# Turning the head-norm output in two halves, and projecting it by halves of its features

## The chip, the core and the metric

The kernel runs on one core of a Trainium2 chip: one TensorE (PE in the profile), one VectorE (DVE), one ScalarE (ACT), one GpSimd (POOL), and one queue (SP) that issues all weight transfers. Time is measured on the device in microseconds (us), from start to end of the program. All arithmetic is in 32-bit floats.

## What is computed

The model is a stack of two blocks on 256 tokens of width 1024. The change touches the mixers of the first block, which run twice (once for each of its two layers). A mixer has two branches, retention and a gated delta rule ("gdn"). In the delta rule a unit lower-triangular system is solved per head. Cut to what matters here:

```python
def mixer_block(h, ...):
    u = rmsnorm(h, g_norm)
    proj = u @ w_in                      # all projections, and two gates mg_ret, mg_gdn
    ...
    y_ret = (o.reshape(B, T, RET_V) * silu(rg)) @ w_br_ret
    ...
    beta = sigmoid(gb)
    g = -exp(a_log) * softplus(ga + dt_bias)
    o = gated_delta_rule(q, k, v, g, beta)                        # 8 heads of 128 features
    o = o * rsqrt(mean(o * o, axis=-1) + EPS) * gdn_gn            # norm of each head
    y_gdn = (o.reshape(B, T, GDN_V) * silu(gz)) @ w_br_gdn        # 1024 x 1024
    merged = sigmoid(mg_ret) * y_ret + sigmoid(mg_gdn) * y_gdn
    return h + merged @ w_out                                     # 1024 x 1024
```

`w_br_gdn` contracts over 1024 features, 128 for each head: features 0 to 511 come from heads 0 to 3, and 512 to 1023 from heads 4 to 7.

## The kernel before

Activations are held transposed, as 8 tiles of 128 features x 256 tokens. Weights stream from memory in slabs of 512 rows x 512 columns (1 MB) through a ring of six (`ring`). PE waits for a slab in `take_slab`; the SP queue issues the transfer of slab n once slab n-6 has been used, in the order of one list (`slab_list`). A projection with transposed output (`linear_t`, matmuls at L413) makes 512 output columns from two slabs: first with features 0 to 511 of the input, then with 512 to 1023. That is 16 matmuls for each slab. Each 32-bit matmul leaves two records in the trace; a transpose leaves one. PSUM is used as four buffers (`ps0` to `ps3`), taken in turn by `take_unit`.

There is no planner: each engine's program is written out by hand, and semaphores tie the engines together. The end of a mixer runs like this:

- `solve_pe`, `solve_dve` and the loops of `mixer_act` and `mixer_pool` handle the heads in two halves of four. For every head n, GpSimd first makes a spread operand (`spread`, L1210: a copy of decay sums and beta over 128 columns into one of two buffers `bc`), PE multiplies it (`spread` at L777 to L780), DVE turns that into a decay mask and the scaled keys (`decay`, L1121 to L1123), and PE makes the Gram matrices (`gram`, L787 to L790). Beside this, PE works through pieces of independent projections (`beside_pe`, L413).
- After the levels of the solve come four short products, u1, r, u2 and o (L833 to L854); each waits for another engine. The last makes the output `o` of four heads in PSUM.
- The head norm follows: ACT squares (L933), DVE sums (L1177) and scales (L1178), GpSimd takes the power -1/2 (L1190), DVE multiplies by it (L1181) and by the gate (L1186) into `o_gdn`. After the second half only, an empty DVE instruction raises `nat_ready`.
- In the second half of the solve GpSimd's first two spread operands stand behind its L1190 of the first half.
- `turn_pe` (L513) then transposes `o_gdn`, 8 transposes for features 0 to 511 and 8 for the rest, into two PSUM buffers. DVE (`turn_dve`, L523) and ACT (`turn_act`, L536) copy one each to `oT`, with the gain. PE waits for both copies.
- PE projects by `w_br_gdn` in two column groups of two slabs each, which DVE gates and adds (`merge_dve`, L1085 and L1087; one `merged_out` for each group). PE waits for both of them, and projects by `w_out`.

`bc` copies wait for `kb_out`, so that a buffer is not overwritten while it is read. The lines named here are the profile's.

Of the kernel before, what the change touches and what calls it, by code (L numbers as in the profile page):

```python
# [14 lines left out]
P = 128  # L15
T = 256
# [98 lines left out]
def build(nc, columns, ins, out, unit_freed):  # L115

    ctx = ExitStack()
    with ctx:
# [64 lines left out]
        u_ready, u_mul, u_shift = sem("u_ready"), sem("u_mul"), sem("u_shift")  # L183
        nat_ready, t_ready_lo, t_ready_hi = sem("nat_ready"), sem("t_ready_lo"), sem("t_ready_hi")
        rope_in, rope_cos, rope_out = sem("rope_in"), sem("rope_cos"), sem("rope_out")
# [8 lines left out]
        hn_sq, hn_ms, hn_rs = sem("hn_sq"), sem("hn_ms"), sem("hn_rs")  # L194
        sig_out, merged_out = sem("sig_out"), sem("merged_out")
        silu_out, hid_out, gate_b = sem("silu_out"), sem("hid_out"), sem("gate_b")
# [36 lines left out]
        def slab_list():  # L233
# [4 lines left out]
            def linear(name, w, c0, width, kt=KT):  # L238
                for j in range(width // 512):
                    for half in range(kt // 4):  # L240
                        wide(name, w, half * 512, 4, c0 + j * 512, 512)

            def ffn(name, e_count):
                slabs.append((name, None, e_count, 0))

            for l in range(DEPTH):
                w = ins["w_in"][l]
                linear(f"rqk{l}", w, OFF_RQ, 1024)
                linear(f"rv{l}", w, OFF_RV, 1024)
                linear(f"rg{l}", w, OFF_RG, 1024)  # L250
                linear(f"gqkv{l}", w, OFF_GQKV, 3072)
                linear(f"gz{l}", w, OFF_GZ, 1024)
                for j in range(2):
                    linear(f"mgret{l}", w, OFF_MR + j * 512, 512)
                    linear(f"brret{l}", ins["w_br_ret"][l], j * 512, 512)
                linear(f"mggdn{l}", w, OFF_MG, D)
                linear(f"brgdn{l}", ins["w_br_gdn"][l], 0, D)
                linear(f"wo{l}", ins["w_out"][l], 0, D)
                if l % 2 == 0:
                    ffn(f"ffn{l}", DENSE_E)  # L260
                    wide(f"ple{l}", ins["w_ple"][l], 0, 2, 0, D)
                    wide(f"pT{l}", ins["p"][l], 0, 2, 0, T)
                else:
                    wide(f"ple{l}", ins["w_ple"][l], 0, 2, 0, D)
                    wide(f"pT{l}", ins["p"][l], 0, 2, 0, T)
                    ffn(f"ffn{l}", EXPERTS)
                linear(f"plg{l}", ins["w_ple_gate"][l], 0, D)
# [124 lines left out]

        def linear_t(pe, slab, unit, src=uT, first=None, early=False, between=None):

            acc = take_unit(pe, unit)
            for half in range(2):
                w = take_slab(pe, slab)
                for m in range(4):
                    mm = linear_t_tile(pe, acc, w, half, m, src, first if m == 0 else None)
                    if between is not None and half == 0 and m % 2:  # L400
                        between[m // 2]()
                    if early and half == 1 and m == 1:
                        mm.then_inc(tick(psum_full), 1)
                        bank_at[unit] = last[0]
                mm.then_inc(tick(slab_used), 1)
            filled(unit)
# [99 lines left out]
        def turn_pe(pe, name, src):  # L506
            pe.wait_ge(nat_ready, T_ORDER.index(name) + 1)
            for half in range(2):
# [5 lines left out]
                mm.then_inc(tick(psum_full), 1)  # L514

        def turn_dve(dve, name, dst, gain, shift=None, same=False):

            unit = f"t0{name}"
            acc = full(dve, unit)
            for k in range(4):  # L520
# [3 lines left out]
                else:  # L524
                    i_ = dve.tensor_scalar(dst[:, k, :], acc[:, k * T:(k + 1) * T], g, shift[:, k:k + 1], ALU.mult, ALU.add)
            i_.then_inc(tick(t_ready_lo), 1)
            free(unit)

        def turn_act(act, name, dst, gain, shift=None, same=False):

            unit = f"t1{name}"
            acc = full(act, unit)
            for k in range(4):
                g = gain[:, 0:1] if same else gain[:, 4 + k:5 + k]
                b = 0.0 if shift is None else shift[:, 4 + k:5 + k]
                i_ = act.activation(dst[:, 4 + k, :], acc[:, k * T:(k + 1) * T], ACT.Identity, bias=b, scale=g)  # L536
            i_.then_inc(tick(t_ready_hi), 1)
            free(unit)
# [126 lines left out]
        def mixer_pe(pe, l):  # L665
# [72 lines left out]
            next_slot[0], ring_pairs[0] = 0, 4  # L738
            turn_pe(pe, f"ogdn{l}", o_gdn)
            pe.wait_ge(t_ready_lo, turned(f"ogdn{l}"))  # L740
            pe.wait_ge(t_ready_hi, turned(f"ogdn{l}"))
            for j in range(2):
                linear_t(pe, f"brgdn{l}", f"brgdn{l}{j}", oT)
            pe.wait_ge(merged_out, 4 * l + 4)
            for j in range(2):
                linear_t(pe, f"wo{l}", f"wo{l}{j}", merged, early=bool(j))

# [5 lines left out]
        def beside_pe(pe, l, i):  # L753
# [4 lines left out]
            if name == "brret" and i % 16 == 8 and j == 0:  # L758
                pe.wait_ge(t_ready_lo, turned(f"oret{l}"))
                pe.wait_ge(t_ready_hi, turned(f"oret{l}"))  # L760
            if i % 8 == 0:
# [95 lines left out]
        def mixer_act(act, l):  # L857
# [54 lines left out]
            for half in range(2):  # L912
# [20 lines left out]
                act.activation(hsqr, full(act, f"o{l}{half}")[:, :], ACT.Square).then_inc(tick(hn_sq), 1)  # L933
            turn_act(act, f"ogdn{l}", oT, col(f"gdn_gn{l}"), same=True)

# [31 lines left out]
        def mixer_dve(dve, l):  # L967
# [96 lines left out]
            for half in range(2):  # L1064
                solve_dve(dve, l, half)
            turn_dve(dve, f"ogdn{l}", oT, col(f"gdn_gn{l}"), same=True)
            for j in range(2):
# [44 lines left out]
        def solve_dve(dve, l, half):  # L1112
# [56 lines left out]
            head_norm_dve(dve, s, f"o{l}{half}", o, hsqr)  # L1169
            if half == 1:  # L1170
                dve.nop().then_inc(tick(nat_ready), 1)

# [19 lines left out]
        def mixer_pool(pool, l):  # L1192
# [5 lines left out]
            for n in range(RET_H):  # L1198
                pool.wait_ge(ret_var, 4 * l + n + 1)
                pool.tensor_tensor(brs, brs, mhalf[:, 0:2], ALU.pow).then_inc(tick(ret_rs), 1)  # L1200
            pool.wait_ge(g_ready, l + 1)
            for half in range(2):
                s = 2 * l + half
                h0 = half * HALF

                def spread(n):

                    if l * GH + n >= 2:
                        pool.wait_ge(kb_out, l * GH + n - 1)
                    pool.tensor_copy(bc[n % 2], gbeta[:, n, :].unsqueeze(2).broadcast_to([P, 4, P])).then_inc(tick(ab_bc), 1)  # L1210

                spread(h0)
                for n in range(h0, h0 + HALF):
# [9 lines left out]
                for lev in range(7):  # L1223
# [5 lines left out]
                    pool.tensor_tensor(CT[:, 0:HALF, :], AT[:, :, 0:P], m, ALU.mult)  # L1229
                    pool.tensor_tensor(CT[:, HALF:8, :], AT[:, :, T:384], m, ALU.mult).then_inc(tick(c_out), 1)  # L1230
                head_norm_pool(pool, s)

# [723 lines left out]
        def hgrn_pe(pe):  # L1956
# [54 lines left out]
            turn_pe(pe, "so0", hg)  # L2011
            pe.wait_ge(t_ready_lo, turned("so0"))
            pe.wait_ge(t_ready_hi, turned("so0"))
            for j in range(2):
# [148 lines left out]
        def attn_pe(pe):  # L2163
# [37 lines left out]
            turn_pe(pe, "so1", ao[0])  # L2201
            pe.wait_ge(t_ready_lo, turned("so1"))
            pe.wait_ge(t_ready_hi, turned("so1"))
            for j in range(2):
# [310 lines left out]
```

## Time and profile before

| | us |
|---|---|
| median of 3 runs | 3118.72 |
| lowest, highest | 3117.86, 3122.47 |
| the profiled execution: its time | 3122.68 |
| its span, first to last instruction | 3120.9 |
| PE busy (matmul) in the span | 2917.6 (93%) |
| DVE, ACT, POOL busy | 736.4, 407.3, 167.5 |
| mean granted clock of TensorE, share of full speed | 0.96 |

The profile is of one execution, whose time is 3.96 us above the median of the three. "Granted clock" is the share of its full rate at which TensorE ran: 1.00 is 2.4 GHz and 0.50 is 1.2 GHz. In rows of the trace a number in square brackets is the idle time of the engine ahead of the row's instructions, and what ended it. The solve and the end of the mixer lie at 205 to 509 us in the first layer and at 967 to 1266 us in the second.

### The profile page before, as it was taken

Reading aid. Unit: us, or ns where it says so; the run is one execution under the profiler, and the core shown is the slowest. Engines: PE = TensorE matmul, PEld = TensorE weight load, DVE = VectorE, ACT = ScalarE, POOL = GpSimd, SP = SyncE. Lnnn points to the kernel's source line nnn. Section 1 sums busy time; section 2 is a strip of 40 time slices with the busy share of each in tenths; the row PEclk is TensorE's granted clock in tenths of the full one; section 3 lists DMA queues with packets and bytes.
Section 4 is the critical chain, followed back from the end, with each engine's and each line's share of the span. In section 5 each row is a group of like instructions: output and inputs, shape, how many; then the busy total and the mean of one; then the engine's idle time right before and its main releaser. Section 6 shows DMA issues by size and latency. Waiting matters only on the chain.

```text
span 3120.9 us, 32663 instructions
## 1 busy us (share of the span) xinstructions
PE 2917.6 (93%) x14182; PEld 2408.1 (77%) x14182; DVE 736.4 (24%) x1275; ACT 407.3 (13%) x615; POOL 167.5 (5%) x154
## 2 busy tenths in 40 slices
PE   7999889999999998999999999797699989996998
PEld 5778777888687887888888877665588877765887
DVE  2333321323243231300000000422322341323001
ACT  1161110001125110100000000220100011121000
POOL 0002210000000230000000000000000010000000
PEclk9999999999999999999999999897799989997999
DMA  6432125766443212444447788241167734331442
GB/s 234 140 128 80 54 68 182 256 250 225 148 135 109 81 54 71 142 149 147 154 156 256 265 286 284 91 160 41 61 244 265 258 110 144 126 108 57 143 156 75
DMA packets 211909, 475.44 MB, mean 152 GB/s; under 512 B 7632, under 2 KB 36944, under 8 KB 211536
## 3 DMA queue, kind: packets, MB, share of 16 engines
q1 hardware_dynamic: 211072, 469.27, 44.3%
q10 hardware_dynamic: 720, 4.46, 0.4%
q8 instruction: 92, 1.51, 0.2%
q14 instruction: 25, 0.20, 0.0%
HBM read 472.64 MB, written 1.05 MB: 152 GB/s over the span
## 4 chain that ended last, share of the span: by engine, by line
PE 84%; issue 10%; DVE 4%; ACT 1%; POOL 1%; DMA 0%; POOLq 0%; DVEq 0%; SPq 0%; ACTq 0%
PE ps L413 27%; PE ps L1289 10%; PE ps L425 10%; PE ps L1470 7%; PE ps L1539 6%; PE ps L1310 5%; PE ps L1490 4%; PE ps L1568 3%; PE ps L816 1%; PE ps L827 1%; PE ps L823 1%; PE ps L2001 1%; PE ps L1986 1%; PE ps L1578 1%; DMA ring<-in_w_in 0%
## 5 line engine op out<-in xcount | busy, mean ns | idle before, releaser
L413 PE MATMUL ps<-uT,ring 128*128 128x256 f32 x2816 | 631.2, 383 | 27.9 <-DMA ring<-in_w_in 16.2
L413 PEld LDWEIGHTS ps<-uT,ring 128*128 128x128 f32 x2816 | 537.0, 192 | 105.3 <-issue 22.0
L1289 PE MATMUL ps<-uT,ring 128*128 128x256 f32 x2112 | 463.9, 382 | 3.2 <-ACT uT L560 2.5
L1289 PEld LDWEIGHTS ps<-uT,ring 128*128 128x128 f32 x2112 | 405.2, 192 | 61.3 <-issue 5.2
L425 PE MATMUL ps<-ring,uT 128*128 128x512 f32 x704 | 305.6, 595 | 0.0
L425 PEld LDWEIGHTS ps<-ring,uT 128*128 128x128 f32 x704 | 133.9, 191 | 164.9 <-issue 164.7
L1310 PE MATMUL ps<-work,ring 128*128 128x256 f32 x1056 | 229.9, 379 | 0.0
L1470 PE MATMUL ps<-uT,ring 128*128 128x256 f32 x1056 | 228.9, 379 | 0.0
L1310 PEld LDWEIGHTS ps<-work,ring 128*128 128x128 f32 x1056 | 200.6, 190 | 27.3
L1470 PEld LDWEIGHTS ps<-uT,ring 128*128 128x128 f32 x1056 | 200.6, 190 | 27.2
L1539 PEld LDWEIGHTS ps<-work,ring 128*128 128x128 f32 x1760 | 198.6, 192 | 5.1 <-issue 4.8
L1539 PE MATMUL ps<-work,ring 128*128 128x128 f32 (+4 forms) x1760 | 198.4, 275 | 0.0
L413 PE MATMUL ps<-xn,ring 128*128 128x256 f32 x768 | 176.0, 389 | 9.5 <-issue 6.8
L413 PEld LDWEIGHTS ps<-xn,ring 128*128 128x128 f32 x768 | 148.6, 196 | 32.1 <-issue 11.7
L1368 DVE TENSOR_TENSOR work<-work,ps 128x1024 f32<-128x1024 f32 (+1 forms) x18 | 20.4, 1132 | 495.6 <-PE ps L1289 495.6
L1490 PE MATMUL ps<-work,ring 128*128 128x256 f32 x528 | 114.9, 379 | 0.0
L1872 DVE SCALAR_TENSOR_TENSOR work<-work 128x1024 f32<-128x1024 f32 x96 | 110.9, 1218 | 0.0
L1490 PEld LDWEIGHTS ps<-work,ring 128*128 128x128 f32 x528 | 100.3, 190 | 13.6
L503 POOL TENSOR_TENSOR tiny<-tiny,small 128x2 f32<-128x2 f32 x15 | 10.5, 697 | 1819.3 <-DVE tiny L493 1819.3
L1568 PE MATMUL ps<-ring,work 128*128 128x512 f32 (+4 forms) x220 | 96.2, 593 | 0.0
L1343 ACT ACTIVATE work<-ps 128x1024 f32<-128x1024 f32 (+1 forms) x18 | 17.2, 953 | 498.2 <-PE ps L1289 498.2
L1724 DVE TENSOR_TENSOR work<-work,ps 128x1024 f32<-128x1024 f32 (+1 forms) x9 | 10.2, 1133 | 292.5 <-PE ps L1470 292.5
(344 smaller groups left out, 2268.7 us busy)
## 6 DMA issues: line engine op xcount, KB each, us to landing
ring<-in_w_in SPq DMA_DIRECT2D x72, 1024.0 KB, 5.0
work<-in_ada_w SPq DMA_DIRECT2D x48, 1024.0 KB, 9.1
ring<-in_exp_w_down SPq DMA_DIRECT2D x40, 1024.0 KB, 4.9
ring<-in_attn_w_in SPq DMA_DIRECT2D x36, 1024.0 KB, 5.1
ring<-in_exp_w_gate SPq DMA_DIRECT2D x32, 1024.0 KB, 5.2
ring<-in_exp_w_up SPq DMA_DIRECT2D x32, 1024.0 KB, 5.3
ring<-in_ffn_w_in SPq DMA_DIRECT2D x32, 1024.0 KB, 5.2
ring<-in_ffn_w_out SPq DMA_DIRECT2D x20, 1024.0 KB, 4.8
```

Of the source, the lines that this page charges most:

```text
L413: mm = pe.matmul(acc[:, m * T:(m + 1) * T], w[:, k, m * P:(m + 1) * P], src[:, half * 4 + k, :], start=(half == 0 and k == 0 and m % 2 == ...
L425: mm = pe.matmul(acc[:, t * 512:(t + 1) * 512], src[:, half * 4 + k, t * P:(t + 1) * P], w[:, k, :], start=(half == 0 and k == 0), stop=(h ...
L816: mm = pe.matmul(acc[:, i * P:(i + 1) * P], CT[:, i, :], X[:, i, :], start=True, stop=True)
L823: mm = pe.matmul(acc[:, i * P:(i + 1) * P], XT[:, i, :], MS[:, i, :], start=True, stop=True)
L827: mm = pe.matmul(acc[:, i * P:(i + 1) * P], MS[:, i, :], XT[:, i, :], start=True, stop=True)
L1289: mm = pe.matmul(acc[:, m * T:(m + 1) * T], w[:, k, m * P:(m + 1) * P], uT[:, half * 4 + k, :], start=(half == 0 and k == 0 and m % 2 == 0 ...
L1310: mm = pe.matmul(bank[2 + n // 4][:, n % 4 * T:(n % 4 + 1) * T], w[:, k, n * P:(n + 1) * P], hid[g][:, t0 + k, :], start=False, stop=True, ...
L1470: mm = pe.matmul(acc[:, m * T:(m + 1) * T], w[:, k, m * P:(m + 1) * P], uT[:, half * 4 + k, :], start=(half == 0 and k == 0 and m % 2 == 0 ...
L1490: mm = pe.matmul(bank[2 + n // 4][:, n % 4 * T:(n % 4 + 1) * T], w[:, k, n * P:(n + 1) * P], hid[g][:, t0 + k, :], start=False, stop=True, ...
L1539: mm = pe.matmul(acc[:, m * c:(m + 1) * c], w[:, k, m * P:(m + 1) * P], picked[:, half * 4 + k, OFFS[i]:OFFS[i] + c], start=(half == 0 and ...
L1568: mm = pe.matmul(bank[1][0:c, n * 512:(n + 1) * 512], hid_picked(i, g)[:, t0 + k, :], w[:, k, n * 512:(n + 1) * 512], start=(g == 0 and t0 ...
L1872: i_ = dve.scalar_tensor_tensor(w, w, 1.0, cond_row, ALU.mult, ALU.mult, accum_out=ada_cols[:, bass.ds(e, 1), c:c + 1].rearrange("p a n -> ...
```

## The change

Three things change in each of the two mixers.

1. **Turning in halves.** The DVE instruction that raises a semaphore after a head norm now stands behind both halves, on `gdn_lo` after heads 0 to 3 and on `nat_ready` after heads 4 to 7. `halves_pe` replaces `turn_pe` and the two `linear_t` for `w_br_gdn`. It transposes features 0 to 511 on `gdn_lo`, lets ACT copy them (`turn_lo_act`), multiplies them into the first column group, transposes the rest on `nat_ready` (DVE copies it, `turn_hi_dve`), and goes through the three other slabs. `slab_list` brings the slabs of `w_br_gdn` in that order. ACT and DVE have exchanged the halves that they copy.
2. **The wait ahead of `w_out`.** It is split: the slab with features 0 to 511 needs the first merged group alone, the next slab the second.
3. **GpSimd's first spread operand.** The copy for the first head of the second half moves from behind the first half's head norm to ahead of it.

```diff
+            def halves(name, w):
+                for half in range(2):
+                    for j in range(2):
+                        wide(name, w, half * 512, 4, j * 512, 512)
...
-                linear(f"brgdn{l}", ins["w_br_gdn"][l], 0, D)
+                halves(f"brgdn{l}", ins["w_br_gdn"][l])
...
-        def linear_t(pe, slab, unit, src=uT, first=None, early=False, between=None):
+        def linear_t(pe, slab, unit, src=uT, first=None, early=False, between=None, ready=None):
             acc = take_unit(pe, unit)
             for half in range(2):
+                if ready is not None:
+                    ready(half)
                 w = take_slab(pe, slab)
...
+        def turn_half_pe(pe, name, src, half):
+            acc = take_unit(pe, f"t{half}{name}")
+            for k in range(4):
+                for t in range(TT):
+                    a = (half * 4 + k) * P
+                    mm = pe.transpose(acc[:, k * T + t * P:k * T + (t + 1) * P], src[:, t, a:a + P], ident)
+            mm.then_inc(tick(psum_full), 1)
+
+        def halves_pe(pe, name, src, lo_ready, lo_n, slab, unit, dst, early=False):
+            pe.wait_ge(lo_ready, lo_n)
+            turn_half_pe(pe, name, src, 0)
+            accs = [take_unit(pe, f"{unit}0")]
+
+            def part(j, half):
+                w = take_slab(pe, slab)
+                for m in range(4):
+                    mm = linear_t_tile(pe, accs[j], w, half, m, dst)
...
+                mm.then_inc(tick(slab_used), 1)
+                if half:
+                    filled(f"{unit}{j}")
+
+            pe.wait_ge(t_by_act, turned(name))
+            part(0, 0)
+            pe.wait_ge(nat_ready, turned(name))
+            turn_half_pe(pe, name, src, 1)
+            accs.append(take_unit(pe, f"{unit}1"))
+            part(1, 0)
+            pe.wait_ge(t_by_dve, turned(name))
+            part(0, 1)
+            part(1, 1)
+
+        def turn_lo_act(act, name, dst, gain):
+            acc = full(act, f"t0{name}")
+            for k in range(4):
+                i_ = act.activation(dst[:, k, :], acc[:, k * T:(k + 1) * T], ACT.Identity, scale=gain[:, k:k + 1])
+            i_.then_inc(tick(t_by_act), 1)
+            free(f"t0{name}")
+
+        def turn_hi_dve(dve, name, dst, gain):
+            acc = full(dve, f"t1{name}")
+            for k in range(4):
+                i_ = dve.tensor_scalar(dst[:, 4 + k, :], acc[:, k * T:(k + 1) * T], gain[:, 4 + k:5 + k], None, ALU.mult)
+            i_.then_inc(tick(t_by_dve), 1)
+            free(f"t1{name}")
...
-            turn_pe(pe, f"ogdn{l}", o_gdn)
-            pe.wait_ge(t_ready_lo, turned(f"ogdn{l}"))
-            pe.wait_ge(t_ready_hi, turned(f"ogdn{l}"))
+            halves_pe(pe, f"ogdn{l}", o_gdn, gdn_lo, l + 1, f"brgdn{l}", f"brgdn{l}", oT)
             for j in range(2):
-                linear_t(pe, f"brgdn{l}", f"brgdn{l}{j}", oT)
-            pe.wait_ge(merged_out, 4 * l + 4)
-            for j in range(2):
-                linear_t(pe, f"wo{l}", f"wo{l}{j}", merged, early=bool(j))
+                linear_t(pe, f"wo{l}", f"wo{l}{j}", merged, early=bool(j),
+                         ready=lambda half: pe.wait_ge(merged_out, 4 * l + 3 + half))
...
             head_norm_dve(dve, s, f"o{l}{half}", o, hsqr)
-            if half == 1:
-                dve.nop().then_inc(tick(nat_ready), 1)
+            dve.nop().then_inc(tick(nat_ready if half else gdn_lo), 1)
...
             pool.wait_ge(g_ready, l + 1)
...
+            spread(0)
             for half in range(2):
...
-                spread(h0)
                 for n in range(h0, h0 + HALF):
...
                     pool.tensor_tensor(CT[:, HALF:8, :], AT[:, :, T:384], m, ALU.mult).then_inc(tick(c_out), 1)
+                if half == 0:
+                    spread(HALF)
                 head_norm_pool(pool, s)
```

The semaphores `t_ready_lo` and `t_ready_hi` are renamed to `t_by_dve` and `t_by_act`, everywhere. How much is computed stays the same.

On PE, at the end of the first layer's solve, the instructions from the last product of `o` on stood like this before. `xn` is the transposed input `oT`, and `ring` the weights; the last row is the first matmul of `w_out`.

```order
L854 MATMUL ps<-work 128x128
L513 MATMUL ps<-small,work 128x128 [waits r_out,nat_ready]
L513 MATMUL ps<-small,work 128x128 x7
L513 MATMUL ps<-small,work 128x128 [waits u_out]
L513 MATMUL ps<-small,work 128x128 x7
L413 MATMUL ps<-xn,ring 128x256 [waits dve_step,slab_in4,t_ready_hi,t_ready_lo]
L413 MATMUL ps<-xn,ring 128x256 x15
L413 MATMUL ps<-xn,ring 128x256 [waits slab_in5]
L413 MATMUL ps<-xn,ring 128x256 [waits slab_in0,sig_out]
L413 MATMUL ps<-xn,ring 128x256 [waits slab_in1]
L413 MATMUL ps<-work,ring 128x256 [waits slab_in2,t_ready_lo,merged_out]
```

The same place now, from the last product on (the lines are those of the changed kernel):

```order
L905 MATMUL ps<-work 128x128
L528 MATMUL ps<-small,work 128x128 [waits r_out,gdn_lo]
L528 MATMUL ps<-small,work 128x128 x7
L420 MATMUL ps<-xn,ring 128x256 [waits slab_in4,t_by_act,u_out]
L420 MATMUL ps<-xn,ring 128x256 x15
L528 MATMUL ps<-small,work 128x128 [waits dve_step,nat_ready]
L528 MATMUL ps<-small,work 128x128 x7
L420 MATMUL ps<-xn,ring 128x256 [waits slab_in5,sig_out]
L420 MATMUL ps<-xn,ring 128x256 [waits slab_in0,t_by_dve]
L420 MATMUL ps<-xn,ring 128x256 [waits slab_in1]
L420 MATMUL ps<-work,ring 128x256 [waits slab_in2,merged_out,t_by_act]
```

The wait for `nat_ready` has moved from ahead of all transposes to behind the first 16 projection matmuls, and the first wait is now for `gdn_lo`.

On GpSimd, at the seam between the two halves of the first layer's solve, this is how it was: the last operand of the levels (L1230), the power of the head norm (L1190), two spread copies (L1210), and the masks of the next head.

```order
L1230 TENSOR_TENSOR work<-work,small 128x512
L1190 TENSOR_TENSOR tiny<-tiny,small 128x8 [waits hn_ms]
L1210 COPY work<-tiny 128x512 [waits kb_out] x2
L1220 TENSOR_TENSOR work<-work,small 128x384 [waits a_out,dec_exp]
L1221 TENSOR_TENSOR work<-work,small 128x384
```

The same seam now, where L1279 is the levels' last operand and L1240 the power:

```order
L1279 TENSOR_TENSOR work<-work,small 128x512
L1256 COPY work<-tiny 128x512 [waits kb_out]
L1240 TENSOR_TENSOR tiny<-tiny,small 128x8 [waits hn_ms]
L1256 COPY work<-tiny 128x512 [waits kb_out]
L1269 TENSOR_TENSOR work<-work,small 128x384 [waits a_out,dec_exp]
L1270 TENSOR_TENSOR work<-work,small 128x384
```

One of the two copies has moved past the power's wait for `hn_ms`; the second still stands behind it.

## Rows read from the trace of the kernel before

**Rows 1.** The page: its first line, and the chain that ended last, by engine.

```profile
span 3120.9 us, 32663 instructions
...
PE 84%; issue 10%; DVE 4%; ACT 1%; POOL 1%; DMA 0%; POOLq 0%; DVEq 0%; SPq 0%; ACTq 0%
```

**Rows 2.** Waits of PE over the run: waiter, releaser, total us, times, longest.

```profile
PE ps L413 <- DMA ring<-in_w_in: 16.2, 1, 16.2
...
PE ps L513 <- DVEq L1171: 13.7, 2, 6.9
...
PE ps L777 <- POOL work L1210: 9.8, 2, 4.9
...
PE ps L413 <- DVE work L1087: 5.2, 2, 2.6
```

**Rows 3.** Timeline, end of the first layer's mixer: start us, us, engine, line, operation.

```profile
425.27 37.96 SPq L2443 DMA_DIRECT2D ring<-in_w_out  x3
...
433.60 1.02 ACT L933 ACTIVATE work<-ps 128x1024 f32<-128x1024 f32 x1 [3.03 <-PE ps L854]
...
436.17 1.64 POOL L1190 TENSOR_TENSOR tiny<-tiny,small 128x8 f32<-128x8 f32 x1 [21.71 <-DVE tiny L1178]
...
439.10 1.22 DVE L1186 TENSOR_TENSOR work<-work 128x1024 f32<-128x1024 f32 x1
...
440.43 3.68 PE L513 MATMUL ps<-small,work 128*128 128x128 f32 x16 [6.86 <-DVEq L1171]
442.44 1.66 DVE L523 TENSOR_SCALAR xn<-ps,small 128x256 f32<-128x256 f32 x4 [2.12 <-PE ps L513]
444.14 1.57 ACT L536 ACTIVATE xn<-ps,small 128x256 f32<-128x256 f32 x4 [9.52 <-PE ps L513]
...
445.81 30.83 PE L413 MATMUL ps<-xn,ring 128*128 128x256 f32 x128 [1.71 <-issue]
...
477.94 1.22 DVE L1087 TENSOR_TENSOR work<-work 128x1024 f32<-128x1024 f32 x1
```

**Rows 4.** Windows: us, busy of PE, PEld, DVE, ACT, POOL, granted clock, DMA share, GB/s.

```profile
336.50:342.40 5.90, 5.88 (x21) 5.34 (x22) 4.02 (x8) 0.95 (x2) 2.41 (x4) 0.50 0.00 0
445.80:476.66 30.86, 30.83 (x128) 26.34 (x128) 2.45 (x2) 0.00 (x0) 0.00 (x0) 0.90 0.30 102
476.66:508.75 32.09, 29.52 (x128) 25.41 (x128) 6.32 (x8) 1.69 (x2) 0.00 (x0) 0.95 0.40 131
1098.97:1103.40 4.43, 4.43 (x17) 4.07 (x17) 2.94 (x5) 0.52 (x1) 0.94 (x2) 0.50 0.00 0
1195.39:1202.26 6.87, 0.01 (x1) 0.01 (x1) 3.84 (x4) 1.02 (x1) 1.64 (x1) 0.79 0.00 0
1207.64:1235.50 27.86, 27.86 (x128) 24.20 (x128) 2.45 (x2) 0.00 (x0) 0.00 (x0) 1.00 0.34 114
1235.50:1265.97 30.47, 27.89 (x131) 24.53 (x131) 7.42 (x12) 1.69 (x2) 0.00 (x0) 1.00 0.03 9
2138.00:2168.40 30.40, 20.21 (x89) 17.35 (x90) 10.57 (x10) 1.02 (x1) 1.64 (x1) 0.50 0.00 1
```

**Rows 5.** The chain in order of time, stretches at full clock: start, us, what.

```profile
916.47 13.81 PE ps L413 x64
...
998.11 1.80 PE ps L513 x16
```

**Rows 6.** Timeline, the seam between the first layer's halves of the solve.

```profile
331.63 1.02 ACT L933 ACTIVATE work<-ps 128x1024 f32<-128x1024 f32 x1 [3.04 <-PE ps L854]
...
335.85 1.17 POOL L1210 COPY work<-tiny 128x512 f32<-128x512 f32 x2
...
337.20 1.22 DVE L1186 TENSOR_TENSOR work<-work 128x1024 f32<-128x1024 f32 x1
...
339.13 0.48 DVE L1121 TENSOR_SCALAR work<-ps,tiny 128x256 f32<-128x256 f32 x1 [0.71 <-PE ps L780]
...
340.95 1.06 PE L787 MATMUL ps<-work 128*128 128x256 f32 x2
```

More of the change, by code:

```diff
@@ L183, in build @@
         u_ready, u_mul, u_shift = sem("u_ready"), sem("u_mul"), sem("u_shift")
-        nat_ready, t_ready_lo, t_ready_hi = sem("nat_ready"), sem("t_ready_lo"), sem("t_ready_hi")
+        nat_ready, t_by_dve, t_by_act = sem("nat_ready"), sem("t_by_dve"), sem("t_by_act")
         rope_in, rope_cos, rope_out = sem("rope_in"), sem("rope_cos"), sem("rope_out")
@@ L194, in build @@
         hn_sq, hn_ms, hn_rs = sem("hn_sq"), sem("hn_ms"), sem("hn_rs")
-        sig_out, merged_out = sem("sig_out"), sem("merged_out")
+        sig_out, merged_out, gdn_lo = sem("sig_out"), sem("merged_out"), sem("gdn_lo")
         silu_out, hid_out, gate_b = sem("silu_out"), sem("hid_out"), sem("gate_b")
@@ L514, in turn_pe @@
                 mm.then_inc(tick(psum_full), 1)
+        def turn_half_pe(pe, name, src, half):
[13 more added lines that the diff above has]
+                    mm = linear_t_tile(pe, accs[j], w, half, m, dst)
+                    if early and half == 1 and j == 1 and m == 1:
+                        mm.then_inc(tick(psum_full), 1)
+                        bank_at[f"{unit}1"] = last[0]
+                mm.then_inc(tick(slab_used), 1)
[22 more added lines that the diff above has]
+            free(f"t1{name}")
         def turn_dve(dve, name, dst, gain, shift=None, same=False):
@@ L525, in turn_dve @@
                     i_ = dve.tensor_scalar(dst[:, k, :], acc[:, k * T:(k + 1) * T], g, shift[:, k:k + 1], ALU.mult, ALU.add)
-            i_.then_inc(tick(t_ready_lo), 1)
+            i_.then_inc(tick(t_by_dve), 1)
             free(unit)
@@ L536, in turn_act @@
                 i_ = act.activation(dst[:, 4 + k, :], acc[:, k * T:(k + 1) * T], ACT.Identity, bias=b, scale=g)
-            i_.then_inc(tick(t_ready_hi), 1)
+            i_.then_inc(tick(t_by_act), 1)
             free(unit)
@@ L758, in beside_pe @@
             if name == "brret" and i % 16 == 8 and j == 0:
-                pe.wait_ge(t_ready_lo, turned(f"oret{l}"))
-                pe.wait_ge(t_ready_hi, turned(f"oret{l}"))
+                pe.wait_ge(t_by_dve, turned(f"oret{l}"))
+                pe.wait_ge(t_by_act, turned(f"oret{l}"))
             if i % 8 == 0:
@@ L933, in mixer_act @@
                 act.activation(hsqr, full(act, f"o{l}{half}")[:, :], ACT.Square).then_inc(tick(hn_sq), 1)
-            turn_act(act, f"ogdn{l}", oT, col(f"gdn_gn{l}"), same=True)
+            turn_lo_act(act, f"ogdn{l}", oT, col(f"gdn_gn{l}").broadcast_to([P, KT]))
         def merge_gate_act(act, l, br, j):
@@ L1065, in mixer_dve @@
                 solve_dve(dve, l, half)
-            turn_dve(dve, f"ogdn{l}", oT, col(f"gdn_gn{l}"), same=True)
+            turn_hi_dve(dve, f"ogdn{l}", oT, col(f"gdn_gn{l}").broadcast_to([P, KT]))
             for j in range(2):
@@ L1201, in mixer_pool, with spread @@
             pool.wait_ge(g_ready, l + 1)
+            def spread(n):
+                if l * GH + n >= 2:
+                    pool.wait_ge(kb_out, l * GH + n - 1)
+                pool.tensor_copy(bc[n % 2], gbeta[:, n, :].unsqueeze(2).broadcast_to([P, 4, P])).then_inc(tick(ab_bc), 1)
+            spread(0)
             for half in range(2):
@@ L1204, in mixer_pool @@
                 h0 = half * HALF
[L1206 to L1210, printed above, removed]
-                spread(h0)
                 for n in range(h0, h0 + HALF):
@@ L2011, in hgrn_pe @@
             turn_pe(pe, "so0", hg)
-            pe.wait_ge(t_ready_lo, turned("so0"))
-            pe.wait_ge(t_ready_hi, turned("so0"))
+            pe.wait_ge(t_by_dve, turned("so0"))
+            pe.wait_ge(t_by_act, turned("so0"))
             for j in range(2):
@@ L2201, in attn_pe @@
             turn_pe(pe, "so1", ao[0])
-            pe.wait_ge(t_ready_lo, turned("so1"))
-            pe.wait_ge(t_ready_hi, turned("so1"))
+            pe.wait_ge(t_by_dve, turned("so1"))
+            pe.wait_ge(t_by_act, turned("so1"))
             for j in range(2):
```

## The prediction

> **What bounds the kernel now.** I read the page first: PE holds 84% of the chain that ended last, and 10% has no releaser that the profile shows [rows 1]. So time can only come from what PE does or waits for. PE's waits over the run give the places: 13.7 us in two waits of 6.9 us ahead of the transposes L513, released by the DVE queue (the empty instruction behind the head norm); 9.8 us in two waits of 4.9 us ahead of L777, released by GpSimd's spread copy; 5.2 us in two waits of 2.6 us ahead of `w_out` [rows 2]. All three come twice, once for each mixer, and the change is at all three. Next came the timeline of the first layer's end, where the reader is to see which engine works while PE stands, and the windows of both layers, which give PE's busy time beside the granted clock.
>
> **The end of a mixer, first layer.** PE's last product of `o` ends when ACT's square starts, at 433.60. Then the head norm runs: square 1.02, DVE, GpSimd 1.64, and DVE's last step from 439.10 for 1.22, and PE starts its 16 transposes at 440.43. DVE's copy (1.66) starts after the first 8, ACT's (1.57) follows the last 8 and ends at 445.71; PE goes on at 445.81, 0.10 later [rows 3]. Then PE takes 30.86 us for `w_br_gdn`, waits for L1085 and L1087 until 479.2, and ends `w_out` at 508.75 [rows 3, 4]. From 433.6 that is 75.15 us.
>
> Now the new order. Durations at full clock: 16 transposes take 1.80 us, so 8 take 0.90; 64 records (two slabs) take 13.81 us, so a slab takes 6.91 [rows 5].
> - Heads 0 to 3 were normed a whole half of the solve earlier: DVE's L1186 of that half ended at 338.42 [rows 6]. So `gdn_lo` costs no wait and the first 8 transposes run from 433.6 to 434.5.
> - ACT has its square until 434.62 and then the four copies, 1.57 us, until 436.2 [rows 3]. PE starts the first slab at 436.3. This is a new stall of 1.8 us, the only new one, and nothing covers it: everything behind it on PE waits.
> - First slab, 6.91 us, until 443.2. Beneath it the head norm of heads 4 to 7 goes on unchanged and is done at 440.3 [rows 3]. It has 2.8 us to spare, so the wait for `nat_ready` goes.
> - 8 transposes until 444.1, and the second slab (features 0 to 511, other columns) until 451.0. It hides DVE's copy of 1.66 us, with 5 us to spare.
> - Two more slabs until 464.8. The first column group is complete at 457.9; its merge (two DVE instructions, 2.5 us from the end of the matmuls to PE's restart in rows 2) ends at 460.4, ahead of `w_out`. The second merge ends at 467.3, while the first slab of `w_out` runs until 471.7. Both halves of the split wait are hidden, the second by 4.4 us.
> - `w_out`, four slabs, 27.6 us: it ends at 492.5 instead of 508.75. Gain 16.3 us.
>
> **Second layer.** The product of `o` ends at 1195.39 and `w_out` at 1265.97, 70.58 us [rows 4]. New length by the same steps: 0.9 + 1.8 + 6.91 + 0.9 + 3 x 6.91 + 27.6 = 58.9 us, hence 1254.3. Gain 11.7 us. The two layers differ because of the clock. In the first `w_br_gdn` and `w_out` take 30.86 and, from 479.2, 29.5 us at granted clocks of 0.90 and 0.95; in the second 27.86 and 27.89 at 1.00 [rows 4]. So 4.6 us of the 16.3 are time that low clock cost this one execution.
>
> Sum for the two ends: 28.0 us.
>
> **The transfers.** The slabs of `w_br_gdn` are all queued ahead of those of `w_out`, and the first issue of the SP row, at 425.27, is already one of `w_out` [rows 3]. PE asks for the first slab 11 us later and for each further one 7 us after the last. The windows of `w_br_gdn` show DMA at 0.30 of its time [rows 4], and PE's waits name a transfer only at the start of the program (16.2 us) [rows 2]. I cost the new order of slabs, and the earlier release of those for the next stage, at nothing. If a slab did come late its whole wait would be PE's.
>
> **The seam of the solve.** At 331.63 ACT's square starts, and PE is through with the first half. GpSimd's two copies come at 335.85 for 1.17 us, PE starts at 336.5 and reaches `gram` (L787) at 340.95, running without a pause behind two spreads. DVE is free at 338.42 but starts L1121 at 339.13, since it waited for PE's L780 [rows 6]. In the new order the first spread runs at once, at 331.6, for about 1 us: the two spreads took 4.4 us from 336.5 to 340.95 at the low clock [rows 6], so one takes half of 2.2 at the full one. The second still comes at 336.5, behind the power. DVE can start L1121 at 338.45, 0.68 earlier, and `gram` then follows its three instructions at 339.6, 1.4 us earlier than 340.95. That would be the gain if the clock were the same. But the clock is 0.50 from 336.5 to 342.4 [rows 4], and now PE enters this stretch with one spread less to do at the low rate, and stands before `gram`. If the clock comes back at the same moment, what is gained is 0.4 us: 1.4 less the 1.0 us of full-clock work that PE otherwise did there. If it comes back as long after the new restart as before (5.9 us after 336.5 in the first layer, 4.4 us after 1098.97 in the second [rows 4]) 1.0 us is lost in each. If PE doesn't drop at all, 1.9 and 1.2 us are gained. So the bounds are -2.1 and +3.1 for both layers. I take 0, near the same-moment case.
>
> **The clock behind the new stall.** The stall of 1.8 us stands between 0.9 us of transposes and the first slab, behind four short products with small waits. The trace has no such stall at this place at full clock, so I bound it. From below: no drop. The wait of 2.58 us ahead of the second layer's `w_out` was followed by 27.89 us at 1.00, no loss. From above: a drop as in the first layer's `w_br_gdn`, 30.86 against 27.6, a loss of 3.2 us a layer; the 2.56 us wait ahead of the first layer's `w_out` cost 1.9 [rows 4]. The new stall is shorter than these two, and one of these two dropped. I allow a third of 2.5 us for each layer, 1.7 in all. The Trainium skill ("TensorE: Matmul & The Clock Gate", Part 1) says that the unit that watches TensorE's activity is not aligned with the program, so that one and the same stall may or may not cost. The two merge waits, nearly equal and of unlike cost, agree; by this rule each end of my bound occurs, in one execution or another.
>
> Total: 28.0 + 0 - 1.7 = 26.3 us. The profiled execution took 3122.68 (span 3120.9 and 1.8 around it) and would take 3096.4. Its first layer paid 4.6 us of clock that the second did not, and it lies 4.0 us above the median of 3118.72. A median run may have paid less there, or elsewhere; the two layers together show the average, so I take the same gain from the median: 3092.4 us.
>
> **Rivals.**
> - *The clock drops at every new place.* For: the low stretches in rows 4. Against: the short stall. Two drops of 3.2 us and the seam at -2.1: 28.0 - 6.4 - 2.1 = 19.5, 3099 us. Chance 0.16.
> - *No drop anywhere, and the seam gives all.* 28.0 + 3.1 = 31.1, 3088 us. Chance 0.12.
> - *The change doesn't do what it says.* If PE's first slab had to wait for the whole head norm after all (because ACT or the semaphore comes late), it could not start before 440.4, later than 436.3 by 4.1 us a layer: 28.0 - 8.2 - 1.7 = 18.1, 3101 us. Against: in the new order ACT has only its square ahead of the copy, and `gdn_lo` is raised 95 us before. Chance 0.03.
> - *Slower: a low clock that stays.* The stall after a few transposes could hold TensorE at 1.2 GHz through the projections. The trace has a stretch of 30 us at 0.50, from 2138 to 2168, where PE is busy 20.2 of 30.4 us in short pieces [rows 4]. Each us of full-clock work costs one more at half rate. The projections are 55.2 us a layer; if all stayed low, the loss would be 110 - 28 = 82 us, 3201 us. It decides once more than 14 us of work a layer runs low. Against: there PE stands a third of the time, while the new order has one stall and then only unbroken matmuls; the first layer's `w_br_gdn`, entered at the low clock, lost 3.2 us in all. Chance 0.01; all else that is slower or equal 0.02.
>
> **How the numbers follow.** The forecast (one drop or none, 24 to 29 us gained) has 0.66, with its own range 3090 to 3095. The range for 8 in 10 takes in both clock rivals partly, and the scatter of single runs (3117.86 to 3122.47, which is what the clock does elsewhere): 3086.5 to 3099.5. About 0.2% (6.2 us) is what a measurement here can tell from no change. All cases but the last give more than that: faster 0.97, same 0.015, slower 0.015.
>
> **What would show it.** In the profile after: PE's waits for the DVE queue of 6.9 us at the mixers' transposes gone, a wait or issue gap of about 1.8 us between the first 8 transposes and the first slab; no wait ahead of `w_out`; from ACT's square of the second half to the end of `w_out` 59 us in each layer, more only where the windows show a clock under 1.00; at the seam, one spread directly after the products and a wait of about 4 us ahead of the next. Wrong would be: the second 8 transposes waiting for `nat_ready`, DMA named as a releaser in the four slabs, or PE at 0.50 through much of the projections.

## The result, and the profile after

| | median us | lowest, highest | runs |
|---|---|---|---|
| before | 3118.29 | 3116.45, 3122.47 | 4 |
| changed | 3095.93 | 3095.35, 3098.33 | 4 |

The ratio of changed to before is 0.9928, with a 95% interval of 0.9911 to 0.9945. The gain is 22.4 us, where 26.3 were forecast; the time lies in the range, 3.5 us above the forecast of 3092.4. The profiled execution took 3095.74 us.

The page of the changed kernel, its first line and the chain by engine, answers to [rows 1]:

```profile
span 3093.9 us, 32669 instructions
...
PE 84%; issue 10%; DVE 4%; ACT 1%; POOL 1%; DMA 0%; POOLq 0%; DVEq 0%; SPq 0%; ACTq 0%
```

PE's share of the chain is the same 84%: it still bounds the kernel, in a span 27.0 us shorter. PE's waits over the run, answering to [rows 2] (waiter, releaser, total us, times, longest):

```profile
PE ps L828 <- POOL work L1256: 7.6, 2, 3.8
...
PE ps L420 <- issue: 6.9, 4, 1.7
...
PE ps L838 <- DVE work L1174: 2.4, 2, 1.7
```

The waits for the DVE queue ahead of the mixers' transposes and those for the merges ahead of `w_out` are gone from the list. At the seam of the solve 3.8 us are left of 4.9 (L828), and a second wait has come up behind it, for DVE's L1174 ahead of `gram` (L838). The timeline of the first layer's end answers to [rows 3]:

```profile
433.15 1.04 PE L528 MATMUL ps<-small,work 128*128 128x128 f32 x8
433.35 1.02 ACT L984 ACTIVATE work<-ps 128x1024 f32<-128x1024 f32 x1 [3.03 <-PE ps L905]
434.27 1.56 ACT L560 ACTIVATE xn<-ps,small 128x256 f32<-128x256 f32 x4
...
435.93 7.14 PE L420 MATMUL ps<-xn,ring 128*128 128x256 f32 x32 [1.74 <-issue]
...
438.84 1.23 DVE L1236 TENSOR_TENSOR work<-work 128x1024 f32<-128x1024 f32 x1
...
442.91 1.04 PE L528 MATMUL ps<-small,work 128*128 128x128 f32 x8
...
443.78 20.89 PE L420 MATMUL ps<-xn,ring 128*128 128x256 f32 x96
443.99 1.66 DVE L567 TENSOR_SCALAR xn<-ps,small 128x256 f32<-128x256 f32 x4 [3.92 <-PE ps L528]
...
459.06 1.23 DVE L1138 TENSOR_TENSOR work<-work 128x1024 f32<-128x1024 f32 x1
...
464.51 3.83 PE L420 MATMUL ps<-work,ring 128*128 128x256 f32 x17
...
465.97 1.22 DVE L1138 TENSOR_TENSOR work<-work 128x1024 f32<-128x1024 f32 x1
```

From the square (L984, 433.35) on, each step is where the forecast put it. The first eight transposes need nothing from this half. The only stall ahead of the first slab is 1.74 us; the profile names no releaser for it, and ACT's four copies (L560) end at 435.83, 0.1 us before the slab starts. The head norm ends at 440.07 under that slab, which ends at 442.9; DVE's copy lies under the second slab, the first merge under the fourth, and the second merge (until 467.2) under the first slab of `w_out`. The windows from the square to the end of `w_out`, in both layers (us, busy of PE, PEld, DVE, ACT, POOL, granted clock, DMA share, GB/s):

```profile
433.35:492.30 58.95, 57.20 (x272) 50.09 (x270) 14.28 (x18) 4.17 (x7) 1.64 (x1) 1.00 0.39 125
1180.00:1238.95 58.95, 57.21 (x274) 50.39 (x273) 15.37 (x22) 4.17 (x7) 1.63 (x1) 1.00 0.18 58
```

Both layers take 58.95 us at a clock of 1.00; 58.9 were forecast, and 75.15 and 70.6 were there before. At the seam of the first layer, answering to [rows 6]:

```profile
331.64 0.60 PE L828 MATMUL ps<-small,work 128*128 128x256 f32 x2
...
336.06 0.61 POOL L1256 COPY work<-tiny 128x512 f32<-128x512 f32 x1
...
336.73 1.22 PE L828 MATMUL ps<-small,work 128*128 128x256 f32 x2 [3.82 <-POOL work L1256]
...
338.80 0.48 DVE L1172 TENSOR_SCALAR work<-ps,tiny 128x256 f32<-128x256 f32 x1 [0.16 <-DVE work L1236]
...
339.92 1.22 PE L838 MATMUL ps<-work 128*128 128x256 f32 x2 [0.69 <-DVE work L1174]
```

The first spread runs directly behind the products, the second waits for GpSimd at 336.06, and `gram` starts at 339.92 after standing again. PE's matmuls there have the length of the low clock: 1.22 us for the two records of L828, against 0.60 for the same two at 331.64.

### The profile page after: what moved, and what is told of

Its sections match the earlier page's. It is cut to its first block, busy times and chain, and to the rows that moved or that the text cites. A ratio compares the mean times of both kernels' runs of the same rounds, so it can differ in the third digit from the quotient of the medians.

```text
span 3093.9 us, 32669 instructions
## 1 busy us (share of the span) xinstructions
PE 2909.2 (94%) x14182; PEld 2405.5 (78%) x14182; DVE 736.5 (24%) x1275; ACT 406.8 (13%) x615; POOL 167.3 (5%) x154
## 4 chain that ended last, share of the span: by engine, by line
PE 84%; issue 10%; DVE 4%; ACT 1%; POOL 1%; DMA 0%; POOLq 0%; DVEq 0%; SPq 0%; ACTq 0%
PE ps L420 27%; PE ps L1340 10%; PE ps L432 10%; PE ps L1521 7%; PE ps L1590 6%; PE ps L1361 5%; PE ps L1541 4%; PE ps L1619 3%; PE ps L867 1%; PE ps L878 1%; PE ps L874 1%; PE ps L2052 1%; PE ps L2037 1%; PE ps L1629 1%; DMA ring<-in_w_in 0%
## 5 line engine op out<-in xcount | busy, mean ns | idle before, releaser
L420 PE MATMUL ps<-uT,ring 128*128 128x256 f32 x2816 | 631.5, 384 | 28.0 <-DMA ring<-in_w_in 16.2
L1541 PEld LDWEIGHTS ps<-work,ring 128*128 128x128 f32 x528 | 100.6, 190 | 13.4
```

The source lines that it names most:

```text
L420: mm = pe.matmul(acc[:, m * T:(m + 1) * T], w[:, k, m * P:(m + 1) * P], src[:, half * 4 + k, :], start=(half == 0 and k == 0 and m % 2 == ...
L1541: mm = pe.matmul(bank[2 + n // 4][:, n % 4 * T:(n % 4 + 1) * T], w[:, k, n * P:(n + 1) * P], hid[g][:, t0 + k, :], start=False, stop=True, ...
```

## The experiments

All times are medians. Each group ran on one chip beside the kernel before, whose time is given with it. The three groups ran on three chips, so times of different groups are best compared by what each gains on the kernel before of its own group.

**First group, before 3117.61 us.** `before_again` is the kernel before, unchanged, for a second profile.

> The kernel before once more, with a new profile. Theory A (the 4.6 us by which the first layer's end was longer than the second's were a low clock of that one execution, not part of the program): from ACT's square (L933) of the second half to the end of w_out, at least one of the two layers stands differently than in the first profile (75.2 and 70.6 us), each between 69 and 75 us, and the difference follows the granted clock. Rival B (the first layer's end is always longer): again 75 and 71 us.

It took 3112.47 us. The windows from the square to the end of `w_out` (columns as above):

```profile
432.34:502.53 70.19, 59.07 (x272) 51.69 (x272) 14.28 (x18) 4.27 (x7) 1.64 (x1) 0.95 0.31 105
1189.10:1259.64 70.54, 59.43 (x274) 52.18 (x275) 15.37 (x22) 4.28 (x7) 1.64 (x1) 0.95 0.14 49
```

70.2 and 70.5 us: the first layer is no longer than the second. The 75.15 us of the first profile came with a longer low clock than this execution had, as theory A said. Over 19 other runs in this group the kernel before took from 3112.93 to 3123.18 us, so this profile is of an execution faster than all of them, and its 70.2 us need not be what a median run has.

`pool_only` has the third part alone, on the kernel before:

```diff
+            spread(0)
             for half in range(2):
...
-                spread(h0)
...
+                if half == 0:
+                    spread(HALF)
                 head_norm_pool(pool, s)
```

> The kernel before with the third part alone: GpSimd's first spread operand ahead of the head norm. Theory A (PE enters the low clock with less work, which takes back what the earlier start gives): 0 to 1 us faster in all, and the profile has PE's waits for GpSimd at 3.8 us, with a second wait for DVE of 0.7 us or more behind. Rival B (the 1.4 us by which gram starts earlier are gained in full): 2.8 us faster.

3119.99 us, ratio 1.0008 (0.9999 to 1.0017): not faster, and 2.4 us slower by the medians, which the interval does not tell from no change. Its waits, and the windows from the first half's square to the second half's in both layers:

```profile
PE ps L777 <- POOL work L1206: 7.6, 2, 3.8
...
PE ps L787 <- DVE work L1123: 1.1, 2, 0.6
```

```profile
332.20:433.77 101.57, 92.29 (x584) 84.51 (x582) 29.83 (x39) 14.95 (x18) 25.48 (x26) 0.97 0.19 63
1091.41:1193.94 102.53, 93.27 (x584) 85.17 (x582) 29.83 (x39) 14.95 (x17) 25.49 (x26) 0.95 0.18 62
```

The wait is shorter, as on the page of the changed kernel, but the stretch is 101.6 and 102.5 us long, against 100.6 and 101.2 in `before_again` and 102.0 and 101.3 in the first profile. Rival B is out. Theory A named the waits rightly (3.8 us, and 0.6 us behind for 0.7) and still expected too much. The ends of the mixers, which this kernel leaves as they were, took 72.2 us (433.77 to 506.01) in the first layer and 70.3 us (1193.94 to 1264.21) in the second.

`split_only` has the second part alone, on the kernel before:

```diff
-            pe.wait_ge(merged_out, 4 * l + 4)
             for j in range(2):
-                linear_t(pe, f"wo{l}", f"wo{l}{j}", merged, early=bool(j))
+                linear_t(pe, f"wo{l}", f"wo{l}{j}", merged, early=bool(j),
+                         ready=lambda half: pe.wait_ge(merged_out, 4 * l + 3 + half))
```

> The kernel before with the second part alone: w_out's first slab waits for the first merged group, its second for both. Theory A: the two merge waits of 2.6 us go, 5.2 us faster, and up to 2 more where the clock had dropped behind them. Rival B (the wait is not PE's to gain, another one takes its place): under 2 us faster.

3111.18 us, ratio 0.9977 (0.9967 to 0.9987): 6.4 us faster, within theory A's 5.2 to 7.2. In its waits the pair ahead of `w_out` is missing and the other two pairs stand as they were:

```profile
PE ps L515 <- DVEq L1173: 13.7, 2, 6.9
...
PE ps L779 <- POOL work L1212: 9.8, 2, 4.9
```

`no_pool` is the changed kernel without its third part (the diff of `pool_only` in reverse).

> The changed kernel with the third part undone: first and second part alone. Theory A: 22 us faster than before, within 1 us of the changed kernel. Rival B (the spread operand first carries part of the gain): 19 to 20 us faster.

3091.09 us, ratio 0.9912 (0.9897 to 0.9927), 26.5 us faster than before. That is more than either theory gave, and 4.8 us below the changed kernel's 3095.93 of the first measurement.

**Second group, before 3118.49 us.** So both were run side by side:

> The changed kernel once more, on one chip with the next three. 22 us faster than before in either theory. It serves as the reference for no_pool_again (is the third part worth less than nothing?) and for the two kernels that fill more of PE's idle time.

> The changed kernel without its third part. Theory A (the spread operand first makes PE enter the stretch at the low clock with less work and stand a second time ahead of gram, so it costs): 1 to 5 us faster than the changed kernel of the same call. Rival B (the third part is neutral, the 4.8 us between the first two measurements came from different chips and the clock's scatter): within 1 us of it.

`after_again` took 3097.83 us (3097.1 to 3098.48), `no_pool_again` 3091.28 (3090.38 to 3092.42). The changed kernel is 6.5 us slower than the same kernel without the third part. That is outside the rival's 1 us, and also more than theory A's 1 to 5. From square to square, first `after_again`, then `no_pool_again`:

```profile
331.13:434.01 102.88, 93.50 (x586) 85.43 (x585) 29.82 (x39) 14.95 (x17) 25.49 (x26) 0.95 0.18 62
1079.13:1181.77 102.64, 93.28 (x586) 85.27 (x585) 29.82 (x39) 14.95 (x17) 25.48 (x26) 0.95 0.19 62
```

```profile
332.64:433.33 100.69, 90.95 (x586) 83.95 (x587) 29.91 (x39) 14.95 (x17) 26.04 (x27) 0.98 0.19 63
1076.77:1177.46 100.69, 90.95 (x586) 83.94 (x587) 29.91 (x39) 14.96 (x17) 26.05 (x27) 0.98 0.19 63
```

4.1 of the 6.5 us (of 7.3 in the spans) lie here. The clock is 0.95 against 0.98, and PE is busy 93.5 and 93.3 us against 91.0 with the same instructions. Over all profiles of kernels that fill neither the seam nor the products, this stretch averages 102.3 us with the spread operand first (ten stretches, 101.5 to 102.9) and 101.2 us without (ten, 100.6 to 102.0): 1.0 us a layer. The granted clock goes with it: 0.95 in five and 0.97 in five of the ten with the spread operand first, 0.97 in seven and 0.98 in three of the ten without. The rest is elsewhere. In a later stage that no part of the change touches, the chain has the first matmuls of the second block's mixer and its transposes at these times (start, us, what), again `after_again` first:

```profile
2099.72 3.57 PE ps L2027 x32
...
2179.75 1.98 PE ps L520 x8
```

```profile
2095.74 3.57 PE ps L2026 x32
...
2172.30 1.98 PE ps L520 x8
```

80.0 us against 76.6, 3.4 us apart. The windows of these two stretches show where they differ:

```profile
2099.72:2179.75 80.03, 52.95 (x288) 45.52 (x288) 26.20 (x23) 3.19 (x4) 3.27 (x2) 0.61 0.03 13
2095.74:2172.30 76.56, 49.48 (x288) 42.80 (x287) 26.20 (x23) 3.19 (x4) 3.27 (x2) 0.66 0.04 13
```

The other engines are busy for the same time in both. PE is busy 3.47 us longer for the same 288 records, at a granted clock of 0.61 against 0.66: the 3.4 us are low clock. `joint_wait`, below, contains the third part too and has 76.7 us:

```profile
2108.30 3.57 PE ps L2027 x32
...
2185.00 1.98 PE ps L520 x8
```

`pool_only`, with the third part alone, has 76.7 us as well, and the kernel before has 80.0 us in its first profile and 78.8 in `before_again`. So these 3.4 us do not hang on the third part as such. The changed kernel had 80.0 us in both its profiles and `no_pool` 76.6 in both; nothing that I ran shows what decides it. `split_only`, `long_norm` and `joint_wait` have 76.7, so a comparison of any of these with the kernel before or the changed one can hold up to 3.4 us that have nothing to do with the edit.

`fill_products` goes on from the changed kernel. It moves the first eight transposes, and ACT's copy of them, ahead of the levels of the second half's solve. It gives the first projection slab's four pieces to PE where it waits between the short products and behind them, and puts the other eight transposes ahead of the last piece of the second slab:

```diff
             mm.then_inc(tick(psum_full), 1)          # x0, second half
+            if half == 1:
+                pe.wait_ge(gdn_lo, l + 1)
+                turn_half_pe(pe, f"ogdn{l}", o_gdn, 0)
...
+            if half == 1:
+                first_slab_pe(pe, l, 0)              # behind u1; 1 behind r, 2 behind u2, 3 behind o
             pe.wait_ge(u_out, 2 * s + 1)
...
+                    if (j, half, m) == (1, 0, 3):
+                        pe.wait_ge(nat_ready, turned(name))
+                        turn_half_pe(pe, name, src, 1)
```

> The changed kernel, with the first eight transposes moved ahead of the first level of the second half's solve, the four pieces of the first projection slab spread between the short products u1, r, u2 and o and behind them, and the transposes of the upper half ahead of the last piece of the second slab. Theory A (every stall of PE at full clock counts in full): the new stall of 1.7 us, the three of 0.7 to 0.8 between the products and 0.9 us of transposes that now lie in another stall go, 4.8 us a layer, 9 to 10 us faster than the changed kernel. Rival B (the solve's chain through ACT and DVE sets the end, so that pieces between the products only delay it): 3.5 us faster, the new stall alone, or less.

3099.19 us, 1.4 slower than `after_again`. Theory A was off by more than 10 us. Rival B's number (3.5 us faster or less) holds, but its reason does not, as `fill_products_free` shows below. The timeline behind the product `o` of the first layer shows why:

```profile
436.44 1.89 PE L420 MATMUL ps<-xn,ring 128*128 128x256 f32 x8
...
440.87 1.23 DVE L1251 TENSOR_TENSOR work<-ps,tiny 128x1024 f32<-128x1024 f32 x1 [1.75 <-POOL tiny L1260]
...
442.15 8.00 PE L420 MATMUL ps<-xn,ring 128*128 128x256 f32 x24 [3.82 <-DVE work L1251]
```

PE stands 3.82 us ahead of the second slab, for DVE's read of `o` (L1251). The transposes had added one unit to the turn of the PSUM buffers, and the second column group got the buffer that held `o`.

`fill_seam` adds the seam to it: four of the pieces that stood beside the second half's heads move behind the first spread.

```diff
             spread(h0)
+            if half == 1:
+                for i in range(24, 28):
+                    beside_pe(pe, l, i)
...
-                for i in range(2):
-                    beside_pe(pe, l, 24 * half + 2 * (n - h0) + i)
+                for i in range(1 if half else 2):
+                    beside_pe(pe, l, 28 + n - h0 if half else 2 * n + i)
```

> As fill_products, and four of the second half's projection pieces moved from the heads to the seam behind the first half, where PE stands for the head norm (one piece a head stays, and four behind the last head). Theory A: PE no longer stands at the seam (3.8 and 0.7 us) and its clock does not drop there (3.4 us more), so up to 8 us a layer and 12 to 16 us faster than fill_products; some is given back if the heads with one piece each wait for GpSimd's masks. Rival B (the heads need their two pieces, and the stall moves there): under 5 us faster than fill_products.

3080.79 us, 18.4 us faster than `fill_products`, above theory A's 12 to 16.

**Third group, before 3116.23 us.** The next two repeat these with one line changed, so that the second group takes another buffer:

```diff
-            next_slot[0], ring_pairs[0] = 0, 4
+            next_slot[0], ring_pairs[0] = 1, 4
```

> fill_products with the second column group's accumulator in another PSUM buffer. In fill_products the extra transposes had shifted the turn of the buffers, the second group got the one that held o, and PE stood 3.8 us a layer until the head norm (L1251) had read it. Theory A (that wait, and the clock that dropped in it, ate the gain): 7.6 us come back, and up to 5 us of clock, so 3087 to 3092 us, 6 to 11 us faster than the changed kernel (3097.8). Rival B (the pieces between the products delay the solve's own chain, and that was the cost): within 2 us of fill_products (3099.2).

> fill_seam with the same mend. Theory A: 7.6 us and up to 4 us of clock less than fill_seam (3080.8), so 3069 to 3074 us. Rival B: within 2 us of it.

3088.01 us (ratio 0.9901, 0.9884 to 0.9917) and 3068.71 us (0.9844, 0.9831 to 0.9858): 11.2 and 12.1 us came back (8.9 and 9.8 when each is measured against the kernel before of its own group), far more than the 2 us of rival B. Theory A had 3087 to 3092 and 3069 to 3074 us; the second time is 0.3 us below its range. `fill_seam_free` is the fastest kernel here, 47.5 us below the kernel before of its group, where the changed kernel is 20.7 to 22.4 below its own. Its stretches from square to square, and the chain behind the product `o`:

```profile
331.39:427.94 96.55, 94.52 (x617) 87.53 (x616) 30.00 (x39) 16.52 (x22) 25.50 (x26) 1.00 0.20 66
1063.81:1160.36 96.55, 94.52 (x617) 87.53 (x616) 30.00 (x39) 16.52 (x21) 25.49 (x26) 1.00 0.19 66
```

```profile
427.90 6.91 PE ps L420 x32
434.81 1.05 PE ps L528 x8
435.85 1.73 PE ps L420 x8
```

At the seam the clock never drops (1.00), and PE is busy 94.5 of 96.55 us. Behind `o` it goes from one slab to the transposes and on, with nothing worth a row between.

`joint_wait` is the changed kernel with its second part undone: both slabs of `w_out` wait for both merged groups again.

> The changed kernel with the second part undone: w_out's first slab waits for both merged groups again. Theory A: the two waits of 2.6 us come back, 5.2 us slower than the changed kernel, and up to 4 more where the clock drops behind them: 3101 to 3107 us. Rival B (with the new order of slabs the merge is hidden anyway): within 1 us of it.

3103.58 us, 5.8 slower than `after_again`, within theory A. (Measured against the kernel before of each group it is 8.0.) From the square to the end of `w_out` its layers take 61.8 us (433.89 to 495.70, clock 1.00) and 63.4 us (1183.81 to 1247.18, clock 0.97), 7.3 us more in sum than the changed kernel's 58.95 each; its later stage, at 76.7 us, gives 3.3 back. The waits of 2.6 us are again there, now under "issue" (four of 1.7 before, six in all):

```profile
PE ps L420 <- issue: 12.2, 6, 2.6
```

`long_norm` lengthens the second half's head norm in the changed kernel:

```diff
+            if half == 1:
+                for _ in range(4):
+                    dstep(dve, dve.tensor_tensor(btmp, hsqr, hsqr, ALU.add))
             dve.nop().then_inc(tick(nat_ready if half else gdn_lo), 1)
```

> The changed kernel with four more DVE operations of 1.25 us in the head norm of the second half, whose results nothing reads. Theory A (the norm is hidden under the first slab with 2.7 us to spare): PE waits 2.3 us a layer for nat_ready, 4.6 us slower than the changed kernel, plus up to 3 us of clock: 3101 to 3106 us. Rival B (the norm still sets the end): 10 us slower or more. Rival C (hidden with far more room): no change.

3102.56 us, 4.7 slower than `after_again`, within theory A's 3101 to 3106. PE waits for the DVE queue again:

```profile
PE ps L528 <- DVEq L1224: 4.3, 2, 2.1
```

2.15 us a layer of the 5.0 us added: 2.85 us of room, for the 2.8 worked out in the prediction.

## Why the prediction was right, and where it was off

- **The ends of the mixers: right.** Both layers came out at 58.95 us for 58.9, with one new stall of 1.74 us for 1.8. Every cover that the forecast named held: the head norm under the first slab with 2.85 us of room (`long_norm`), DVE's copy, and both merges. The merge waits are worth 5.2 us in two waits of 2.6; `split_only` gained 6.4 us and `joint_wait` lost 5.8, both with some clock in them.
- **The transfers: right.** The only transfer that PE's waits name is the one of 16.2 us at the start of the program, as before, and the second to fourth slab run without a pause (20.89 us for 96 records, 443.78 to 464.5).
- **The new stall's clock: 1.7 us allowed, none seen.** In both layers of both profiles of the changed kernel the end ran in 58.95 us, within 0.01, at a clock of 1.00.
- **The same gain from the median: the step that was off.** From the profiled execution the sum holds: 3096.4 us was forecast and 3095.74 measured, and the spans differ by 27.0 us, of which 27.8 lie in the two ends (16.2 + 11.6). But that execution paid 4.6 us more in the first layer, and I carried it whole to the median of other executions, saying that they may have paid elsewhere. The first layer's end took 75.15 us there, 72.2 in `pool_only` and 70.2 in `before_again`; the second layer's took 70.3 to 70.6 in all three. From the shortest the gain is 11.2 + 11.6 = 22.8 us, not 28.0. What a median run pays there is not shown.
- **The spread operand first: taken as 0, and by most signs it costs.** The prediction gave both directions, -2.1 to +3.1 for both layers, and took a value near the middle. The means over twenty stretches differ by 1.0 us a layer, which is the lower bound, and `pool_only` was 2.4 us slower by the medians, in an interval that just includes no change. PE took less work into the low clock, as the prediction reasoned, and the low clock did not end sooner for it: the granted clock of the stretch fell (0.95 or 0.97 against 0.97 or 0.98). In size that is the case of "as long after the new restart", not the one of "at the same moment".
- **Luck.** The 1.7 us taken off for a clock that did not drop made up for part of what the ends and the spread operand gave less. Without it the forecast would have been 5.2 us off, still in the range.

22.8 - 2.0 = 20.8 us. The changed kernel gained 22.4 in the first measurement and 20.7 in the second, and 1.7 us between these is within what the kernel before scatters. `no_pool` has 22.8 by these steps, and 26.5 and 27.2 measured. The clock of the later stage fills most of this: 76.6 us there, against 80.0 and 78.8 in the two profiles of the kernel before, is 2.2 to 3.4 us more. Why the clock differs there stays open.

## What to carry to other kernels

A projection can start on the half of its input that was ready long before, if the weights come in that order and the accumulators are open side by side; count what lies beneath each slab, and the gain is the stall less the copy that is newly exposed. Making one operand earlier helped nothing here, since the engine stood again behind it; work for the whole wait, which kept the clock at 1.00 at the seam (`fill_seam`, `fill_seam_free`), gained 18.4 us over `fill_products`. Before a sum is taken from a profile, look in it for stretches at low clock that a second profile may not have. And before a difference of a few us is put down to an edit, compare the stages that the edit doesn't touch: here one of them differed by up to 3.4 us.

## What had not been expected

- The same instructions from square to square kept PE busy for 91.0 us at a mean clock of 0.98 and for 93.5 at 0.95. What the traces show to differ at the low clock is one spread less there and one stall of 0.6 to 1.7 us more.
- A stage of the second block took 76.6 us or 80.0 us in kernels that differ only 1000 us earlier, by the granted clock alone. Two kernels kept their value in both their profiles; the kernel before did not (80.0 and 78.8). The times of the changed kernel and of `no_pool` lay within 1.4 to 3 us in each group, where those of the kernel before spread over 10; `split_only`, `fill_seam` and `fill_products_free` spread over 4.8 to 6.5.
- One more unit in a rotation of three PSUM buffers moved a wait of 3.8 us a layer into a place that had none, and cost 9 to 12 us in all with the clock.
